# A two-layer encoder trunk on one core: one routing test per layer, a ring of nine weight slots, and an output projection that frees its weights by block

## The reference

```python
for i in range(DEPTH):
    hn = rms_norm(h, mix_norm_g[i])
    mix = ...                      # even: RG-LRU | sparse attention; odd: retention; then @ w_out
    h = h + mix
    h = h + hier_moe(rms_norm(h, ffn_norm_g[i]), ...)
    e = rms_norm(p[i] @ ple_w_up[i], ple_norm_g[i])
    h = h + e * sigmoid(h @ ple_w_gate[i])

def hier_moe(x, ...):
    g_sel = argmax(xf @ w_group)                       # one of 4 groups
    top_vals, top_idx = top_k(within, 2)               # two of its 8 experts
    for e in range(32):
        hid = silu(xf @ w_gate[e]) * (xf @ w_up[e])    # 1024 -> 512
        out = out + combine[:, e:e + 1] * (hid @ w_down[e])
```

## Time and profile before

| | us |
|---|---|
| median of 3 runs | 1496.6 (1495.3 to 1498.16) |
| the profiled execution, its own time | 1501.17 |
| its span | 1499.3 |
| TensorE matmuls busy | 1133.1 (76%) |
| VectorE, ScalarE, GpSimd busy | 329.2, 161.4, 102.9 |
| main DMA queue, packets' share of 16 engines | 75.9% |
| moved | 474.80 MB, mean 317 GB/s |

### The profile page before, as it was taken

The page is one execution under the profiler, slowest core; times in us unless marked ns, Lnnn a source line. Parts: engine busy times, 40 slices in busy tenths (PEclk is TensorE's granted clock), DMA queues, the critical chain, the costliest instruction groups (busy, mean ns, idle before and its releaser), DMA issues.

```text
span 1499.3 us, 27512 instructions
## 1 busy us (share of the span) xinstructions
PE 1133.1 (76%) x10854; PEld 655.7 (44%) x10855; DVE 329.2 (22%) x809; ACT 161.4 (11%) x380; POOL 102.9 (7%) x230
## 2 busy tenths in 40 slices
PE   6999867666676767568999999977666767666658
PEld 5884434344343434334444554434343434343333
DVE  1496221111111111112110441131111111111111
ACT  1224201000000000001001000110000000000000
POOL 0010010000000000000110000010000000000000
PEclk9999979888888888879999999979888888888889
DMA  9731369999999999993534321379999999999970
GB/s 364 279 134 63 127 240 424 429 427 429 430 428 428 429 430 428 429 401 142 199 113 168 113 84 56 117 313 406 428 428 428 429 428 428 429 429 428 428 326 28
DMA packets 56393, 474.80 MB, mean 317 GB/s; under 512 B 3832, under 2 KB 5880, under 8 KB 31520
## 3 DMA queue, kind: packets, MB, share of 16 engines
q1 hardware_dynamic: 55008, 469.27, 75.9%
q10 hardware_dynamic: 1056, 3.89, 0.7%
q0 software_dynamic: 288, 1.05, 0.2%
HBM read 473.12 MB, written 3.16 MB: 318 GB/s over the span
## 4 chain that ended last, share of the span: by engine, by line
PE 44%; DMA 40%; issue 7%; DVE 6%; ACT 1%; SPq 1%; POOL 0%; DVEq 0%; ACTq 0%; POOLq 0%
DMA ring<-in_moe_w_up_dram 39%; PE ps L696 14%; PE ps L504 12%; PE ps L527 11%; PE ps L495 2%; PE ps L485 1%; PE ps L713 1%; DMA ring<-in_ev_w_in_dram 1%; DVE arena L1165 1%; SPq L414 1%; PE ps L721 1%; PE ps L663 1%; PE ps L671 0%; DVE arena L1182 0%; DVE arena L1146 0%
## 5 line engine op out<-in xcount | busy, mean ns | idle before, releaser
L696 PE MATMUL ps<-ring,arena 128*32 128x256 f32 x4096 | 348.1, 512 | 232.0 <-issue 232.0
L696 PEld LDWEIGHTS ps<-ring,arena 128*32 128x32 f32 x4096 | 191.0, 145 | 384.4 <-issue 358.6
L1365 DVE SCALAR_TENSOR_TENSOR arena<-arena,ps 64x256 f32<-64x256 f32 x64 | 26.4, 413 | 774.0 <-ACT arena L984 774.0
L504 PE MATMUL ps<-ring,xT 128*128 128x512 f32 x416 | 184.1, 600 | 4.7 <-DVE arena L1244 3.5
L713 PE MATMUL ps<-ring,arena 128*32 128x256 f32 x2048 | 124.1, 382 | 46.8 <-DVE arena L1376 46.8
L504 PEld LDWEIGHTS ps<-ring,xT 128*128 128x128 f32 x416 | 79.6, 193 | 100.1 <-issue 95.7
L713 PEld LDWEIGHTS ps<-ring,arena 128*32 128x32 f32 x2048 | 61.1, 109 | 96.2 <-DVE arena L1376 58.0
L721 PE MATMUL ps<-arena 32*128 32x256 f32 x1024 | 73.3, 398 | 38.0 <-ACT arena L995 38.0
L984 ACT ACTIVATE arena<-ps 64x256 f32<-64x256 f32 x64 | 24.1, 377 | 676.9 <-PE ps L696 676.9
L721 PEld LDWEIGHTS ps<-arena 32*128 32x128 f32 x1024 | 49.5, 184 | 67.0 <-issue 67.0
L495 PE MATMUL ps<-xT,ring 128*128 128x256 f32 x320 | 73.3, 392 | 2.0 <-DMA ring<-in_ev_w_in_dram 2.0
(11 more groups left out here) (195 smaller groups left out, 711.2 us busy)
## 6 DMA issues: line engine op xcount, KB each, us to landing
ring<-in_moe_w_gate_dram SPq DMA_DIRECT2D x64, 2048.0 KB, 17.2
ring<-in_moe_w_up_dram SPq DMA_DIRECT2D x64, 2048.0 KB, 21.6
ring<-in_moe_w_down_dram SPq DMA_DIRECT2D x64, 2048.0 KB, 23.2
ring<-in_od_w_in_dram SPq DMA_DIRECT2D x12, 2048.0 KB, 9.3
ring<-in_ev_w_in_dram SPq DMA_DIRECT2D x6, 2048.0 KB, 21.2
ring<-in_ple_w_gate_dram SPq DMA_DIRECT2D x4, 2048.0 KB, 16.1
ring<-in_od_w_out_dram SPq DMA_DIRECT2D x4, 2048.0 KB, 7.9
ring<-in_ev_w_out_dram SPq DMA_DIRECT2D x2, 2048.0 KB, 13.5
```

The costliest lines, as they stand in the source:

```text
L504: ins = nc.tensor.matmul(b, xT[:, k, t * P:(t + 1) * P], w[:, k, :], start=k == 0, stop=k == KD - 1)
L696: ins = nc.tensor.matmul(ps[TOK * i:TOK * i + TOK, 5, 0:2 * P].rearrange("p (b n) -> p b n", b=2), rows_[:, k, :], w[i // 2][:, k, i % 2], ...
L1365: ve.scalar_tensor_tensor(out=th[0:2 * TOK].rearrange("p b n -> p (b n)"), in0=th[0:2 * TOK].rearrange("p b n -> p (b n)"), scalar=1.0, in ...
```

## The change

Five things are changed.

1. **One test per layer.** VectorE keeps the largest count of the layer (`most`) instead of all counts. TensorE, ScalarE, VectorE and GpSimd each load it once and take one of two whole paths: all 32 experts with one chunk of 32 rows (the first case), or all with eight chunks. In the first case semaphores are raised by eight at once. GpSimd, which had no test, now waits for this count before its first pick. On TensorE the transposes of h and the gate matmuls (`after`) stand in both paths.
2. **Nine slots for experts.** `ring` and `arena` become one tensor `big`; its slots 0 to 5 are the ring, slots 6 to 9 and a tail of 2336 floats the arena. Experts rotate over three sets of three slots (`EXPERT_SLOTS`), of which slots 7, 8 and 9 are arena memory. The small tiles of the experts move into `xT`, the diagonals into the second half of `xn`, the squares of the embedding into their PSUM bank. SyncE waits for the arena (`arena_free`) before the first block that goes there. `up{l}` has the tail of the arena, loaded after that wait. TensorE has experts 0 and 1 as straight code and experts 2 to 31 in a loop of three.
3. **Blocks freed one by one.** `out0`, `rout0`, `rout1` and `rout2` raise `block_read` as soon as their last matmul has run.
4. **Gain rows earlier.** `gain{l}` moves from the mixture layer to a place ahead of `out1` and of the odd output projection; its transpose on VectorE moves with it, ahead of the additions into h.
5. **By token tile after the experts.** h is transposed one token tile after the other, and the gate matmuls run token tile by token tile over both weight blocks.

```diff
@@ Loads
-        self.order = ["iq", "q", "xa", "k", "ga", "v", "out0", "out1"]
...
+        even = [("iq", 0), ("q", 1), ("xa", 2), ("k", 3), ("ga", 4), ("v", 5), ("out0", 0), ("out1", 1)]
+        odd = [("gate0_0", 7), ("gate0_1", 9), ("rq0", 0), ("rq1", 1), ("rk0", 2), ("rk1", 3), ("rv0", 4), ("rv1", 5),
+               ("rv2", 0), ("rv3", 1), ("rg0", 2), ("rg1", 3), ("rg2", 4), ("rg3", 5)]
+        odd += [(f"rout{c}", c) for c in range(4)]
+        self.plain = [even, odd, [("gate1_0", 1), ("gate1_1", 2)]]
...
+EXPERT_SLOTS = [[[2, 3, 4], [5, 9, 8], [0, 7, 1]], [[4, 5, 9], [8, 7, 0], [1, 2, 3]]]
@@ SyncE
+        BLOCK_READ = {"out0": 1, "rout0": 2, "rout1": 3, "rout2": 4}
...
+            def arena_free(l):
+
+                if l:
+                    full(sync, "yT3_1")
+                else:
+                    taken(sync, "logit1_3")
...
-                for e in range(2):
+                for e in range(DEPTH):
                     for kind in range(3):
-                        slot_free(m0 + 3 * e + kind)
-                        expert(l, m0 + 3 * e + kind, kind, e)
-                with sync.Fori(0, NE // 2 - 1) as it:
...
+                        i = EXPERT_SLOTS[l][e][kind]
+                        if i == NSLOT - 1:
+                            arena_free(l)
+                            plain(f"up{l}")
+                        if i < RING:
+                            slot_free(i)
+                        elif i == RING + 1 and l == 0:
+                            full(sync, "pv1")
+                        expert(l, kind, e, e)
+                for e in range(DEPTH, DEPTH + 2):
+                    for kind in range(3):
+                        expert_read(l, kind, e - DEPTH)
+                        expert(l, kind, e, e % DEPTH)
+                with sync.Fori(0, (NE - DEPTH - 2) // DEPTH) as it:
...
@@ TensorE
+                    if blk in BLOCK_READ:
+                        ins.then_inc(block_read, 1)
...
             taken(pe, "pv1")
+            gain_rows(0)
             outs(lambda k, t: ybT[:, k - 4, t * P:(t + 1) * P], "out1", 4, 8)
...
+                def step(e, n, j):
+
+                    u, p = units(l, e), pick_units(l, e)
+                    pe.wait_ge(xe_ready, u + UNITS)
+                    gate_up(n, j, UNITS)
+                    gather(p + 2 * UNITS, UNITS)
+                    pe.wait_ge(share_ready, done(l, e) + UNITS)
+                    turn_share(UNITS)
                     pe.wait_ge(hidT_ready, u + UNITS)
+                    down(n, j, UNITS)
                     pe.wait_ge(share_taken, u + UNITS)
                     pe.wait_ge(y_taken, u + UNITS)
-                    combine(last)
+                    combine(UNITS)
...
+                def experts(one):
+
+                    for e in range(2):
+                        one(e, 0, e)
+                    with pe.Fori(0, (NE - 2) // DEPTH) as it:
+                        for j in range(DEPTH):
+                            one(it * DEPTH + 2 + j, it + (2 + j) // DEPTH, (2 + j) % DEPTH)
+
+                def after():
+
+                    for t in range(NT):
+                        pe.wait_ge(h_ready, NT * (3 * l + 1) + t + 1)
+                        for c in range(2):
+                            transposes(f"hT{l}_{t}{c}", [h[:, t, k * P:(k + 1) * P] for k in range(4 * c, 4 * c + 4)])
+                    for t in range(NT):
+                        for c in range(2):
+                            taken(pe, f"hT{l}_{t}{c}")
+                        rows(f"gate{l}", lambda k, t: xT[:, k, t * P:(t + 1) * P], [f"gate{l}_0", f"gate{l}_1"], 4, (t,))
...
+                count = pe.value_load(most[0:1, l:l + 1], min_val=0, max_val=S)
+                at = next_job[0]
+                with pe.If(count < TOK + 1):
+                    gather(pick_units(l, 0) + UNITS, UNITS)
+                    experts(step)
+                    after()
+                with pe.Else():
+                    next_job[0] = at
+                    experts(chunks)
...
@@ VectorE
-                emptied(f"count{l}", ve.tensor_copy(counts[0:1, :], cb[0:1, 0:NE]))
+                emptied(f"count{l}", ve.tensor_reduce(most[0:1, l:l + 1], cb[0:1, 0:NE], AX, ALU.max))
...
+                    dve.wait_ge(combined, UNITS * NE * (l + 1))
                     ve.tensor_tensor(hq, hq, ps[:, 0:QUARTERS, t * QD:(t + 1) * QD], ALU.add).then_inc(h_ready, 1)
@@ GpSimd
-                pool.wait_ge(rk_ready, l + 1)
-                pick_rows(0)
...
+                pool.wait_ge(info_ready, l + 1)
+                count = pool.value_load(most[0:1, l:l + 1], min_val=0, max_val=S)
+                with pool.If(count < TOK + 1):
+                    pick_rows(0, iota[:, 1:1 + TOK], done(l, 0) + UNITS, UNITS)
```

More of the change, by code:

```diff
@@ L530, in part, with gain_rows @@
                                 end(job, ins)
-                return part
+                    if blk in BLOCK_READ:
+                        ins.then_inc(block_read, 1)
+                return part
+            def gain_rows(l):
+                b = begin(f"gain{l}")
+                pe.wait_ge(dgain_ready, l + 1)
+                for q in range(QUARTERS):
+                    ins = nc.tensor.matmul(b[TOK * q:TOK * q + TOK, 0:QD], ones[:, 0:TOK], dgain[:, 2 * q:2 * q + 2, :],
+                                           start=True, stop=True)
+                end(f"gain{l}", ins)
             def norm_transposes(name, count, src):
@@ L649, in moe @@
                 embed(0)
-                b = begin(f"gain{l}")
-                pe.wait_ge(dgain_ready, l + 1)
-                for q in range(QUARTERS):
-                    ins = nc.tensor.matmul(b[TOK * q:TOK * q + TOK, 0:QD], ones[:, 0:TOK], dgain[:, 2 * q:2 * q + 2, :],
-                                           start=True, stop=True)
-                end(f"gain{l}", ins)
                 norm_transposes(f"ffnT{l}", (xn_ready, NT * (2 * l + 2)), xn_t)
@@ L766, in moe @@
                 pe.wait_ge(info_ready, l + 1)
-                pe.wait_ge(pick_ready, NE * l + 1)
                 for name in (f"up{l}_11", f"count{l}", f"up{l}_01", f"up{l}_10"):
                     taken(pe, name)
-                gather(pick)
-                n0 = loads.moe[l]
-                with pe.Fori(0, NE // 2 - 1) as it:
-                    for u in range(2):
-                        step(it * 2 + u, n0 + 3 * u, it)
-                step(NE - 2, n0 + 3 * (NE - 2), 0)
-                step(NE - 1, n0 + 3 * (NE - 1), 0, last=True)
```

516 lines of the change are left out of this document (250 added, 266 removed).

## The result

The changed kernel takes 1437.0 us in the median (four runs, 1435.9 to 1438.8), the kernel before beside it 1496.1 (1495.3 to 1498.2). The ratio is 0.9597, 95% interval [0.9583, 0.9612]: 59.0 us less, where the sum of the forecast was 53.8 (1443 us). The sign, the mechanism of the large terms and the range held; the sum was 5 us short. The profiled execution took 1437.69 us with a span of 1435.9, against 1501.17 and 1499.3 before, so the two traces differ by 63.4 us.

The account below looks back on a forecast made before the run. The kernel was taken as bound in turn by TensorE and DMA (mixture layers by DMA). Terms of -30.9 us in layer 0 and -22.9 in layer 1, together -53.8, gave a 1443 us median, range 1433 to 1458.

Parts of the forecast that it names:

- T0, layer 0: Moment the first expert's gate/up matmuls end, releasing the first slot: GpSimd's count wait +1.8, expert 0's test -5.5, so -3.7 us.
- T0 to expert 31, layer 0: From the first slot release to the last expert's first matmul: 425.0 us instead of 451.2, so -26.2 us.
- gate matmuls to T0 of layer 1: Between the mixture layers: +1.0 us for gain rows before the output projection, -0.2 us for the tests before expert 0.
- T0 to expert 31, layer 1: Same stretch in the second mixture layer: 425.0 us instead of 447.7, so -22.7 us.
- The ring: Nine blocks loaded before the first slot release instead of six: three transfers of 4.89 us fewer, 14.7 us per layer.
- The tail: Last experts inside the loop without per-expert tests: stops before expert 31 go, about 11 and 7 us in the two layers.
- I add +1.0 per layer: Code behind the expert loop, first met with DMA loaded, costs +1.0 us per layer (bounds 0 and 5.8).
- the 2.0 us gain beside it: After the experts, adding and transposing h by token tile brings the gate matmuls 2.0 us earlier in each layer.
- the wait for the diagonals: Before layer 1's output projection TensorE waits for VectorE's diagonals, then runs the gain rows: 1.6 - 0.6, so +1.0 us.
- The stops move: Rival, 20%: fetching code after the loop costs 5.8 us twice and the first pass loses DMA time; about +10, 1453 us.
- The new slots fill no earlier: Rival, 5%: some wait in SyncE's order stands ahead of the new slots' loads; 29.4 us go, 1472 us.
- The larger loop does not stay in instruction memory: Rival, 3%: each expert's code in TensorE's loop is fetched anew, 16.0 us per expert, +49 per layer, 1590 us.

Follow-up runs that it names:

- tail_jumps: Changed kernel with experts 29 to 31 as straight code behind the loop, each after an unused expert block that is jumped over: 1446.7 us, ratio 0.9662 to the kernel before.
- loop_of_6: Changed kernel with six experts per pass of TensorE's loop (five passes) in place of three: 1447.9 us, ratio 0.9683 to the kernel before.
- untested: Changed kernel without any test of the largest count, only the path with one chunk on all four engines: 1434.7 us, ratio 0.9574 to the kernel before.
- freed_at_end: Changed kernel without block_read, so out0 and rout0 to rout2 are freed at the end of their projection: 1437.2 us, ratio 0.9587 to the kernel before.
- tail_outside: Changed kernel with experts 29 to 31 as straight code behind the loop of three, without any test: 1438.2 us, ratio 0.959 to the kernel before.
- two_tiles: Changed kernel with the old order after the experts, both token tiles added, transposed, then multiplied together: 1444.3 us, ratio 0.9634 to the kernel before.
- ring_six: Changed kernel with SyncE waiting as if only six expert slots existed: 1466.8 us, ratio 0.9782 to the kernel before.
- loop_of_15: Changed kernel with 15 experts per pass of TensorE's loop (two passes) in place of three: 1453.2 us, ratio 0.97 to the kernel before.
- run 13: Not a run's label: "run" is a verb here, saying the loops of six and fifteen experts take 13 and 15 us longer than the changed kernel.

## Why the prediction was right

By its own steps, in us, forecast against the two traces (which differ by 63.4):

| step | forecast | shown |
|---|---|---|
| T0, layer 0 | -3.7 | -2.2 |
| T0 to expert 31, layer 0 | -26.2 | -26.0 |
| expert 31 to the gate matmuls, layer 0 | -1.0 | -4.2 |
| gate matmuls to T0 of layer 1 | +0.8 | -3.0 |
| T0 to expert 31, layer 1 | -22.7 | -22.5 |
| expert 31 to the gate matmuls, layer 1 | -1.0 | -3.8 |
| from there to the end | 0 | -1.7 |
| sum | -53.8 | -63.4 |

**The large terms held, and by their causes.** The ring: 14.7 forecast, 14.9 and 14.8 in the run with six slots. The tail: 11 and 7 forecast, 11.1 and 7.5 in the kernel before without tests. The last step of this, that jumps stop TensorE and code in line does not, stands on two runs: straight code without jumps (no stop), and with them (5.86 and 5.10 us).

**T0** came 2.2 us earlier. The start of the program is 1.9 us later (the load that waits for the value product goes out at 136.09 for 134.22). That is no part of the change: the nine other profiled versions of the changed kernel have this load between 131.8 and 136.5. Against that, T0 gained 4.1, for 3.7 forecast. TensorE in order of time:

```profile
195.31 1.93 PE L738 MATMUL ps<-xn,xT 128*32 128x256 f32 x16 [2.45 <-POOL xT L1622]
198.43 6.11 PE L752 MATMUL ps<-big,xT 128*32 128x256 f32 x64 [1.18 <-DVE xT L1416]
```

The wait for GpSimd before the gather grew from 1.33 to 2.45 us: the count load and its branch cost 1.1 us, for 1.8 forecast. From the gather's start to the matmuls 3.12 us pass, for 8.42 before.

**The step that failed: "I add +1.0 per layer" after the experts, and the 2.0 us gain beside it.** No stop came there: at most 0.13 us of "issue" at a time, although that code is also met for the first time; it is in line, and the run with straight experts shows what that means. I had the rule in hand (the stops follow jumps) and did not apply it. And the split by token tile saves 3.3 us, not 2.0: I had left 1.3 us for the later tile's additions and copies, which run under the transposes. That is 2.3 of the 3.2 us that layer 0 missed by. The other 0.9 lies between expert 31's start and the addition (11.3 for 12.2), which the prediction had taken as unchanged, and 0.5 of it in expert 31's own gate/up matmuls (5.38 for 5.90). In layer 1 the two came to 2.9 (3.63 for 6.50) and 0.9 us (11.15 for 12.06).

**Terms that were missing.** Between the layers, the wait for the diagonals came out about as forecast (from the gate matmuls to the odd output projection 1.3 us more, for 1.6). The projection itself took 1.5 us longer (granted clock 0.97 for 1.00), the way from the addition into h to the transposes 1.5 less, GpSimd's test 1.1 more, and expert 0's own stop, 1.8, went, and 0.7 more from its first matmul to T0. But 3.4 us went where nothing was changed: the logits and the second embedding tile after the odd mixing take 3.73 + 3.51 us (L713, L571), for 4.78 + 5.81 (L663, L527). The same matmuls in the same number are faster, with a granted clock of 0.97 from 933 to 952. The kernel before had 0.85 there (963 to 987 us), and the loop of fifteen, at 0.74, needed 5.99 + 6.25. So this is the clock's, and of no part of the change: in the runs that leave this code alone the same two groups take 7.24 us (`tail_jumps`, `loop_of_6`, `untested`), 8.94 (`freed_at_end`, `tail_outside`, `two_tiles`), 10.58 (`ring_six`) or 12.24 (`loop_of_15`). A forecast can't have this term, and that the trace after had the shortest of these times is luck. At the end, 1.7 us went, which I had counted at 0, and this too is clock. The 64 gate matmuls of layer 1, before:

```profile
1464.65 29.41 PE ps L527 x64
```

They take 27.72 us after, and the same 27.72 in the run with the old order after the experts, so it is not the order by token tile. Before, the granted clock is 0.68 in their first 5.35 us; after, it is 1.00 throughout. The kernel before without tests has 29.59 and all runs of the changed kernel have 27.72, so here the difference does go with the kernel; why TensorE's clock is lower there is open.

**Profiled execution and median.** 4.6 us of the 63.4 are the profiled execution of before, which was that much above its median; the one of after was 0.7 above. By medians the sum was 5 us short.

**The rivals.** "The stops move" did not come: between the last landing and the gate matmuls no "issue" is over 0.14 us. "The new slots fill no earlier" did not come: nine blocks are out 33 and 30 us before T0. It would not have taken the early freeing to avoid it, as the run without that shows. "The larger loop does not stay in instruction memory" was wrong for three experts, but its cause is real: the loops of six and fifteen do not stay, or not reliably, and run 13 and 15 us longer by the ratio. Its price was far off, since only the jump back stops TensorE and not each expert. The Trainium skill (Runtime: NRT & Kernel Launch, section Instruction fetch mechanics) gives "no instruction cache" as the rule: no packet in 360 us of looping over three experts speaks against it. The same section of the Trainium skill says that a taken branch whose target is outside the current window of two pages forces a fetch before execution goes on; the traces agree for jumps over code that was not there yet (idle times of 5.1 to 5.9 us ahead of experts 29 and 30 while the weight queues are full), and not for the jump back of the loop of three, which fetches nothing.

## What to carry to other kernels

When a stage waits for transfers, count blocks and not the busy share: each block that is in before the stage's first release is its whole transfer time less, and it matters only that they are all in, not when each went out. On the engine that leads at the end of such a stage, keep rare cases out of line, one branch for the stage and not one per item, because a jump over unfetched code cost a stop of some 5 us here, which the last items could no longer hide. Keep a loop's code short enough to stay loaded: here three experts per pass were, six were not reliably. And before a difference of a few us is put down to an edit, compare the stages that the edit left alone.

## What the hardware did that I had not expected

**How much code stays.** The loop of fifteen fetched 30 packets, 0.49 MB in all, in 360 us, that is in 24.5 steps: an estimate of 20 KB per expert. By this, the loop of three has some 60 KB and never fetches, the one of six 120 KB and fetches in one layer and nearly not in the other, the one of fifteen 300 KB and always fetches. The limit so lies between 60 and 300 KB, and the unsteady loop of six suggests near 120. The Trainium skill (Runtime: NRT & Kernel Launch, section Instruction fetch mechanics) gives 128 KiB for TensorE, which agrees with the estimate. Why the loop of six came to rest after some passes is open.

**Code in line does not stop TensorE, even under full load.** In the loop of fifteen every expert's code is fetched while DMA is at 427 GB/s, and TensorE stops for it only at the jump back (5.58 us in layer 0, 0.5 of them lost in the end). It is not free for all that: most of the 6.2 us that each layer loses there lies in steps in which the weights land late. Three experts' code met once, as in the run with the straight tail, cost nothing.

**The same short stretch at many clocks.** The logits and the second embedding tile after the odd mixing took between 7.24 and 12.24 us in kernels whose code is the same there, with granted clocks of 0.97 and 0.74 around them at the two ends. A difference of 5 us between two such traces is thus not to be put down to an edit without a look at the granted clock.
